# Two modulation tiles behind each of the 24 gates of layer 0's merge, in place of 32 of them around the choice of experts

## What is computed

```python
for l in range(DEPTH):                                   # 2 layers
    mod = silu_c @ w_ada[l] + b_ada[l]                   # 1024 x 6144, for the latents
    modc = silu_cc @ w_ada[l] + b_ada[l]                 # and for the context
    ...
    x = x + gt1 * latent_mixer(p, ctx_kv, ...)           # 512 positions; ends in merge_branches
    h2 = modulate(rmsnorm(x, g_ffn[l]), sh2, sc2)
    x = x + gt2 * expert_choice_ffn(h2, w_router[l], w_e_gate[l], w_e_up[l], w_e_down[l])
    if not last:                                         # layer 0: 256 positions of context as well
        ...

def merge_branches(o_a, o_b, o_c, gate_logits, w_branch, w_out):
    g_a, g_b, g_c = jnp.split(jax.nn.sigmoid(gate_logits), 3, axis=-1)
    merged = g_a * (o_a @ w_branch[0]) + g_b * (o_b @ w_branch[1]) + g_c * (o_c @ w_branch[2])
    return merged @ w_out

def expert_choice_ffn(h, w_router, w_g, w_u, w_d):       # 16 experts
    aff = jax.nn.softmax(logits, axis=1)
    gate, idx = lax.top_k(aff, cap)
    xs = h[bi, idx]                                      # gathered rows
    ...
```

## Time and profile before

| | us |
|---|---|
| median of 3 runs (3526.8 to 3530.91) | 3527.5 |
| the profiled execution | 3523.05 |
| its span | 3521.2 |
| PE busy in the span | 3275.4 (93%) |
| DVE busy | 1241.1 (35%) |
| ACT busy | 1004.2 (29%) |
| POOL busy | 225.4 (6%) |

### The profile page before, as it was taken

The page is one execution under the profiler, slowest core; times in us unless marked ns, Lnnn a source line. Parts: engine busy times, 40 slices in busy tenths (PEclk is TensorE's granted clock), DMA queues, the critical chain, the costliest instruction groups (busy, mean ns, idle before and its releaser), DMA issues.

```text
span 3521.2 us, 48003 instructions
## 1 busy us (share of the span) xinstructions
PE 3275.4 (93%) x21250; PEld 2200.7 (62%) x21250; DVE 1241.1 (35%) x1821; ACT 1004.2 (29%) x1571; POOL 225.4 (6%) x142
## 2 busy tenths in 40 slices
PE   6999999999699999989999996988879999989998
PEld 4787667888334343467768882332328766858887
DVE  3335642233401011145563333111125444353333
ACT  3623541122210001037353222000022354342223
POOL 0100000121100000001000220000002010120000
PEclk9999999999799999999999998999999999989999
DMA  7540014222899999833102329999983121323331
GB/s 216 148 146 25 1 49 121 66 61 60 322 397 398 389 351 389 313 63 82 43 1 71 97 91 366 421 421 421 422 329 85 36 59 37 96 60 97 101 96 66
DMA packets 385614, 617.00 MB, mean 175 GB/s; under 512 B 99234, under 2 KB 288896, under 8 KB 360704
## 3 DMA queue, kind: packets, MB, share of 16 engines
q1 hardware_dynamic: 378064, 596.50, 48.0%
q0 software_dynamic: 4384, 15.73, 1.3%
q10 hardware_dynamic: 2960, 1.71, 0.2%
HBM read 606.54 MB, written 7.34 MB: 174 GB/s over the span
## 4 chain that ended last, share of the span: by engine, by line
PE 81%; DMA 10%; DVE 4%; ACT 3%; issue 1%; POOL 0%; ACTq 0%; SPq 0%; DVEq 0%
PE ps L592 33%; PE ps L1843 6%; PE ps L2227 5%; PE ps L1083 4%; DMA ring<-in_w_e_up 4%; PE ps L1172 3%; PE ps L1846 3%; DMA ring<-in_w_e_down 3%; PE ps L1879 3%; PE ps L1133 3%; PE ps L644 3%; PE ps L1347 3%; PE ps L1838 2%; PE ps L613 2%; PE ps L1884 2%; PE ps L1875 2%
## 5 line engine op out<-in xcount | busy, mean ns | idle before, releaser
L592 PE MATMUL ps<-xh,wh 128*128 128x512 f32 x1912 | 638.1, 372 | 19.2 <-DVE xl L2073 9.3
L592 PE MATMUL ps<-xl,wh 128*128 128x512 f32 x1912 | 630.4, 368 | 0.0
L592 PE MATMUL ps<-xh,wl 128*128 128x512 f32 x1912 | 630.1, 367 | 0.0
L565 DVE TENSOR_TENSOR wl<-ring,wh 128x1024 fp32r<-128x1024 f32 (+1 forms) x259 | 332.1, 1283 | 443.6 <-ACT wh L556 441.8
L592 PEld LDWEIGHTS ps<-xh,wh 128*128 128x128 f32 x1912 | 330.4, 189 | 101.3 <-issue 23.8
L556 ACT ACTIVATE wh<-ring 128x1024 fp32r<-128x1024 f32 (+1 forms) x259 | 272.0, 1051 | 421.2 <-PE ps L592 161.8
L592 PEld LDWEIGHTS ps<-xh,wl 128*128 128x128 f32 x1912 | 330.4, 189 | 61.2
L592 PEld LDWEIGHTS ps<-xl,wh 128*128 128x128 f32 x1912 | 330.1, 189 | 58.6 <-issue 0.5
L1843 PE MATMUL ps<-ring,arena 128*32 128x512 f32 x1344 | 176.6, 597 | 0.9 <-ACT arena L1592 0.9
L1838 PE MATMUL ps<-ring,arena 128*64 128x512 f32 x704 | 161.7, 602 | 11.7 <-DMA ring<-in_w_e_up 7.1
L1094 DVE TENSOR_REDUCE sm<-ps 128x2 f32<-128x1536 f32 (+3 forms) x96 | 142.3, 1482 | 41.8 <-PE ps L1083 41.4
(11 more groups left out here) (277 smaller groups left out, 4440.0 us busy)
## 6 DMA issues: line engine op xcount, KB each, us to landing
ring<-in_w_e_gate SPq DMA_DIRECT2D x87, 1024.0 KB, 19.5
ring<-in_w_e_up SPq DMA_DIRECT2D x85, 1024.0 KB, 19.9
ring<-in_w_e_down SPq DMA_DIRECT2D x85, 1024.0 KB, 20.9
ring<-in_w_in SPq DMA_DIRECT2D x112, 512.0 KB, 4.1
ring<-in_w_ada SPq DMA_DIRECT2D x96, 512.0 KB, 5.0
arena<-in_w_e_up SPq DMA_DIRECT2D x43, 1024.0 KB, 18.7
arena<-in_w_e_down SPq DMA_DIRECT2D x43, 1024.0 KB, 20.0
arena<-in_w_e_gate SPq DMA_DIRECT2D x41, 1024.0 KB, 21.0
```

Source lines behind the costliest of these rows:

```text
L565: e.tensor_tensor(in_heads(X, u, m.WL[:, o:o + many]), heads_of(X, u, halves.aps[s], many), in_heads(X, u, m.WH[:, o:o + many].bitcast(F32 ...
L592: i = e.matmul(ps[0:M, a:b], w[:, k, 0:M], h[:, k, a:b], start=k == 0 and p == 0, stop=k == 7 and p == 2)
```

## The change

All 48 tiles of groups 3 to 5 are multiplied in the merge, two behind each of the 24 gates (behind the branch products where the gate has them). Groups 3 and 4 are turned ahead of gates 8 and 16, group 5 ahead of the third tile of the output projection. ACT's copies of the groups stand behind the sigmoids of gates 7, 15 and 23. The choice holds no modulation work any more, `MR` is one buffer, and the loads are in the order of use.

```diff
-        MR = lambda pair: tmp[:, 3840:4352] if pair < 4 else AR(21504, 512)
+        MR = tmp[:, 3840:4352]
...
                     if d % 2 == 0:
                         gate(t + 1)
-                    if t < 8:
-                        mods(48 + 2 * t)
                     if d % 2:
                         X.split(("b", br, d), 256, branch(l, br, d - 1, 256))
                         if t < 23:
                             gate(t + 1)
-                    if t < 8:
-                        mods(49 + 2 * t)
+                    mods(48 + 2 * t, 49 + 2 * t)
             for d in range(KD):
                 X.split(("o", d), 128, column(I["w_out"][l], 128 * d))
-            mods(*range(64, 96))
...
-                    if l == 0 and t == 8:
-                        pe_modt(e, 3)
+                    if l == 0 and t in (8, 16):
+                        pe_modt(e, 2 + t // 8)
                     pe_linear3(e, X, ("g", br, d), 128, T, (X.key, "g", t), g_sg.at(X.key, t))
-                    if l == 0 and t < 8:
-                        pe_mod(e, 48 + 2 * t)
...
-                    if l == 0 and t < 8:
+                    if l == 0:
+                        pe_mod(e, 48 + 2 * t)
                         pe_mod(e, 49 + 2 * t)
             for d in range(KD):
+                if l == 0 and d == 2:
+                    pe_modt(e, 5)
...
-            if l == 0:
-                for m in range(64, 68):
-                    pe_mod(e, m)
             pe_total(e, f"f{l}", KD, T, tmp[:, 2304:3072], sqr[0])
...
                     e.activation(work[t % 5][:, 0:T], bank.of[X.key, "g", t][:, 0:T], ACT.Sigmoid).then_inc(*g_sg.up(X.key, t))
-                    if l == 0 and t == 7:
-                        act_mod(e, 3)
+                    if l == 0 and t % 8 == 7:
+                        act_mod(e, 3 + t // 8)
                     if d % 2:
                         act_high(e, X, X.unit["b", br, d] + 1)
...
-                    if l == 0 and t == 8:
-                        dve_mod(e, 3)
+                    if l == 0 and t in (8, 16):
+                        dve_mod(e, 2 + t // 8)
...
             for d in range(KD):
+                if l == 0 and d == 2:
+                    dve_mod(e, 5)
                 dve_low(e, X, X.unit["o", d] + 1)
...
-            mods(*range(68, 80))
...
-            mods(*range(80, 88))
...
-            if l == 0:
-                pe_modt(e, 4)
...
-            mods(*range(88, 96))
-            if l == 0:
-                pe_modt(e, 5)
```

## The result

The changed kernel takes 3546.1 us (median of 6 runs, 3545.08 to 3548.38) beside 3527.15 for the kernel before (6 runs, 3524.08 to 3530.91): ratio 1.0053, interval 1.0042 to 1.0064. It is slower by 19 us; the forecast was 3548.

The account below looks back on a forecast made before the run. PE was taken to bound the merge and experts, while the choice had slack. Terms +20.5, +5.2, +10.4, +0.8 and -16.5 gave +20.4 us on the 3527.5 median: 3548 us, range 3535 to 3558.

Parts of the forecast that it names:

- visits in the merge: Behind the merge's gates: 16 new two-tile visits at 1.36 us, less 1.2 saved at the first eight; +20.5 us.
- stop at gate 16: In the merge: PE stops while ACT copies a group ahead of the high half, then slow products; +5.2 us, low bound 3.0.
- stop at the output projection: Before w_out: the last group's copy delays ACT's xh tiles, and PE waits; +10.4 us, 8.2 if the clock holds.
- last group's transposes, and the pace of `w_out`: Output projection: the last group's transposes stand before w_out's third tile; +0.8 us, between nothing and 1.4. No pace change forecast.
- the choice: From output projection's end to first gathered rows: removing the modulation tiles gives back time; -16.5 us in all.
- rival 2: Stop at w_out is hidden because ACT's and DVE's pieces overlap otherwise; +10.0, 3537.5 us, chance 0.13.
- Router: In the choice: its result comes sooner without mods waiting for w_ada; 3.4 us back, 2.9 to 3.9.
- Folding product: In the choice: eight mods no longer stand between the copied router result and the folding products; 7.6 us back.
- index: In the choice: the index is turned at once, without mods 94 and 95, a copy and four transposes ahead; 3.5 us back.
- The gather: End of the choice: waits less for DMA with four loads beside it, not seven; 1.0 us back, 0 to 3.1.
- Rival 1: DMA paces layer 0's experts, so seven early weight tiles give back 18.4 us; +2, 3530 us, not slower; chance 0.07.
- Rival 3: In the merge: the six-slot ring doesn't keep up, new visits wait for w_ada; 14 us more, 3562; chance 0.07.

Follow-up runs that it names:

- the fifth experiment: Kernel before with ACT's copy of group 3 behind the high half of gate 8's next weights, transposes behind gate 8's products; 3524.4 us, ratio 0.9993.
- the first experiment: Changed kernel with ACT's copy of group 5 moved between the sixth and seventh xh tile of the output projection; 3534.89 us, ratio 1.0028.
- the third: Changed kernel with the 48 tiles in twelve visits of four behind the odd gates; 3544.55 us, ratio 1.0053 to the kernel before.
- the fourth experiment: Changed kernel with all loads of layer 0's experts held until the product that turns the index; 3547.87 us, ratio 1.0061 to the kernel before.
- the sixth: Kernel before with tiles 80 to 87 behind the normed rows' transposes, 88 to 95 behind the index products, under the gather; 3529.15 us, ratio 1.0008.
- seventh: Kernel before with the edits of the fifth and sixth together, and tiles 64 to 79 two by two behind gates 8 to 15; 3529.89 us, ratio 1.0006.
- the second: Changed kernel with group 5's copy moved, groups 3 and 4 copied behind the next high half, transposed behind gates 8 and 16; 3528.76 us, ratio 1.0006.
- eighth experiment: Against the kernel before: 36 tiles in the merge in nine visits of four, no stops, twelve in PE's idle time of the choice; 3516.4 us, ratio 0.9972.

## Why the prediction was right, point by point

The terms, in us, each against what the two traces show:

| term of the sum | forecast | measured |
|---|---|---|
| visits in the merge | +20.5 | +20.3 |
| stop at gate 16 | +5.2 | +4.5 |
| stop at the output projection | +10.4 | +9.7 |
| last group's transposes, and the pace of `w_out` | +0.8 | +1.6 |
| the choice | -16.5 | -15.4 |
| sum | +20.4 | +20.6 |

The sum is closer than its terms: two stops 0.7 too dear each and the visits 0.2, against 0.8 and 1.1 on the other side. The mechanism is as said place by place, but that the errors cancel to 0.2 is luck.

**The visits.** Steps of 27.83 against 27.8 said. The 20.3 are the growth from first to last sigmoid, 324.52 - 301.15 = 23.4, less gate 16's stop of 4.5, and 1.4 for the visit behind gate 23. Gate 8's own step, 22.38, is 0.5 shorter than before, where the joined visit makes it 0.3 shorter; this lies in the 20.3.

**The stop at gate 16.** 22.62 - 18.16 = 4.5 where 5.2 were said. The term was mis-sized by a step of its working: "0.83 the visit". In the kernel before, two visits of one tile lie between the sigmoids of gates 7 and 8, the one at 605.68 and this one, from the timeline of PE before:

```profile
596.45 0.64 PE L665 MATMUL ps<-ring,cs 128*32 128x256 f32 x8
```

So the same step without the stop is 18.47, as the fifth experiment shows, and gate 8's stop cost 4.4 us, 3.0 of gap and 1.4 of slow products, not 2.2. That second part comes and goes: over the same step without a stop, gate 16 costs 4.5 in the changed kernel, 2.9 in the first experiment (21.06 - 18.15) and 3.1 in the third (22.05 - 19.00, with four tiles in the visit). For those two the low bound of 3.0 was the better figure.

**The stop at the output projection.** From the last sigmoid to the first product of `w_out` it is 849.19 - 829.98 = 19.21 where it was 9.93: 9.3 more, 1.4 of it the visit, so 7.9 (8.2 said). The first tile takes 10.43 against 8.60, 1.8 (2.2 said, the figure misread at gate 8). The first experiment took both away by moving the copy and won 10 us. This was shown, not only read from the rows; rival 2 (the stop hidden) falls.

**Transposes and pace.** The step with the transposes is 8.93, 0.45 over its neighbours. The other 1.1 were not foreseen: all tiles of `w_out` take 8.48 in this trace and 8.32 before.

**The choice.** Norm 1.0 as said. Router 2.9 of the 3.4: the result came 1.57 behind ACT's last tile, where 1.0 was taken. Folding product 7.5 of 7.6, index 3.5, and 1.3 that weren't in the sum, as the folding product took 1.48, at a granted clock of 1.00 (938.0 to 939.5), and not the 2.75 of the earlier trace rows, at 0.50. The gather is the one step of wrong sign: 0.7 given away where 1.0 was to be given back. The step that failed is "four loads are nearer to seven than to none": the fourth experiment has nine loads at the gather and 8.93 us, the changed kernel four and 9.00. The number of loads beside it isn't what sets it, and layer 1's 5.2 us was no measure for layer 0's gather.
The Trainium skill, page "DMA: Bandwidth & Descriptors", section "Issuing engines are not separate DMA queues", says that transfers of SP and GpSimd run on the same 16 engines and interleave. The prediction took from it 8.31, unchanged, and a sum of +21.4. The measured 9.00 is nearer to that than to the 7.3 of the forecast, but 0.7 above it, and no run here shows the interleaving to be the cause.

**The other rivals.** Rival 1 (experts paced by DMA): the leads of seven loads were given and, in the fourth experiment, taken away, with no effect on the stage beyond 0.8 us (603.65 and 602.89), 0.6 of which lie between its first two gathered products, where PE waits for no weight. It is PE. Where the loads lose 10 us more, as in the sixth and seventh, the rival comes true: the point lies between a first load 10 us ahead of the first gathered product (fourth experiment, 960.08 to 970.38) and 2.3 us ahead. Rival 3 (the ring): no product waited for w_ada in the merge.

The forecast of 3548 was the sum on top of the median of 3527.5. The medians lie 19.0 apart, the traces 20.6 up to the first gathered product and 23.0 with the experts; differences of this size lie within what the last section shows of chance.

## What to carry to other kernels

An operation that waits for the end of a piece of work must not stand ahead of what the next piece needs, on an engine that runs in order: one 0.6 us copy cost 10 us in front of `w_out`. Filler work belongs in the idle time of the engine that does it, with its data in the ring before; taken from there to where that engine is the bound, it pays in full (1.36 us a pair) whatever its old place gives back. And what stands behind the filler in the queue of loads must still arrive: when the last tiles went under the gather, the 10 us won at the index were gone by the eighth gathered product.

## What the runs showed of the hardware that wasn't expected

**A short gap may or may not cost clock.** The traces hold ten stops of 3 us at a gate. Over the same step without a stop, five of them cost 2.9 to 3.1 us, the gap and no more (both of the first experiment, both of the third, the one of the sixth), and five cost 4.2 to 4.6 (the one before, both of the changed kernel, both of the fourth experiment), with slow products behind the gap. The first products do not always tell: in the fourth experiment two take 0.59 right behind the gap of gate 8, and the clock falls 1 us later, as PE's timeline shows:

```profile
609.22 0.59 PE L588 MATMUL ps<-xh,wh 128*128 128x512 f32 x2 [1.58 <-DVE wl L561]
...
611.19 0.84 PE L588 MATMUL ps<-xl,wh 128*128 128x512 f32 x2
...
614.35 0.52 PE L588 MATMUL ps<-xl,wh 128*128 128x512 f32 x2
```

At the end of layer 0's experts all kernels have the same two small gaps of 1.86 and 0.83 us; windows around them, in the kernel before and in the fifth experiment:

```profile
1480.00:1500.00 20.00, 17.31 (x194) 6.95 (x195) 2.40 (x4) 1.64 (x4) 0.00 (x0) 1.00 0.48 191
```

```profile
1480.00:1500.00 20.00, 17.31 (x166) 6.14 (x162) 1.71 (x3) 1.25 (x3) 0.00 (x0) 0.83 0.34 134
```

The piece from the last of layer 0's gathered products to the first product of layer 1's values takes 139.9 us in four traces (before, the second, seventh and eighth experiment), 141.5 or 141.6 in four (the changed kernel, the first, third and fourth) and 143.8 in two (the fifth and sixth). In the 10 us behind the first of the two gaps the granted clock is 1.00 in the first four, 0.83 in the next four and 0.66 in the last two. From the second gathered product on, the steps from one to the next agree to 0.05 us in all traces but those of the sixth and seventh experiment. Of the 2.3 us that the experts' stage is longer in the changed kernel 1.5 are this, and 0.8 lie between its first two gathered products (10.02 against 9.22), where the clock starts at 0.50 and PE waits for no weight in either. Differences of a profile under 4 us can't be put down to an edit by themselves.

**Two paces at full clock.** A tile of `w_out` takes 8.32 us in the traces of before, the fifth and the seventh experiment and 8.48 in the others (in the first experiment only from the third tile's end on, its second takes 8.32), with a granted clock of 1.00 in both; in the slower, one record of two wide products in three reads 0.53 where the faster has 0.51 or 0.52. What decides it stays open: the merge and output projection of the sixth experiment are those of the kernel before.

**The gather.** 8.31 and 8.36 us in the chain for the kernel before and the fifth experiment, 8.81 to 9.15 in the changed kernel and the first four experiments and the eighth, whether four or more loads start beside it. The cause of these 0.6 us stays open too.
